# Feed-forward of an encoder block by a Strassen scheme: seven half-size products for eight, in two phases

## The reference, cut to what matters

```python
h = x + mixer(rmsnorm(x, norm1_g))              # attention and gated linear attention: not changed
n = rmsnorm(h, norm2_g)
gate = conv3(n @ w_gate) + conv_b               # depthwise over 3 neighbouring rows
h = h + (silu(gate) * (n @ w_up)) @ w_down      # w_gate, w_up 2048x5632, w_down 5632x2048
out = rmsnorm(h, final_norm_g)
```

## Time and profile before

| | |
|---|---|
| median of 3 runs | 2384.5 us (2384.22 to 2385.77) |
| span of the profiled execution | 2383.3 us (no other time of that execution is given) |
| PE busy | 98% of the span |
| DVE, ACT, POOL busy | 41%, 30%, 2% |
| DMA | 222.43 MB, mean 93 GB/s |
| last matmul of the mixer starts | 913.12 us |
| first feed-forward slab starts | 923.06 us |

### The profile page before, as it was taken

One profiled execution on the slowest core, in us unless ns is written; L12 is line 12 of the kernel. 1 busy time (PEld: TensorE's weight loads), 2 busy tenths in 40 slices (PEclk: granted clock), 3 DMA queues, 4 the chain that ended last, 5 costly groups with the idle time before them and its releaser, 6 DMA issues.

```text
span 2383.3 us, 26573 instructions
## 1 busy us (share of the span) xinstructions
PE 2340.9 (98%) x10613; PEld 1916.7 (80%) x10613; DVE 975.3 (41%) x1333; ACT 719.1 (30%) x930; POOL 39.7 (2%) x48
## 2 busy tenths in 40 slices
PE   6999999999999999999999999999999999999997
PEld 5887888887777787888888888888888888888886
DVE  4223444643564436343343434343433434343434
ACT  5224443423343233331222222221312222222214
POOL 1000000000000000000000000000000000000002
PEclk9999999999999999999999999999999999999999
DMA  5332212222242232333333232333333323223233
GB/s 174 98 96 82 62 54 71 63 79 80 80 150 67 75 97 73 114 98 97 97 97 95 94 95 96 96 97 97 97 97 97 97 97 95 94 95 95 96 97 106
DMA packets 113488, 222.43 MB, mean 93 GB/s; under 512 B 6862, under 2 KB 9140, under 8 KB 112788
## 3 DMA queue, kind: packets, MB, share of 16 engines
q1 hardware_dynamic: 111684, 215.07, 29.0%
q0 software_dynamic: 1744, 6.52, 0.8%
HBM read 217.37 MB, written 4.19 MB: 93 GB/s over the span
## 4 chain that ended last, share of the span: by engine, by line
PE 96%; ACT 1%; DVE 1%; DMA 1%; issue 0%; SPq 0%; ACTq 0%; DVEq 0%
PE dense L508 59%; PE side L508 30%; PE side L681 1%; PE side L664 1%; PE side L628 1%; PE side L624 1%; PE side L546 1%; DMA xin<-in_x 1%; PE side L671 1%; PE side L611 1%; PE side L568 0%; PE side L592 0%; PE side L640 0%; ACT L910 0%; PE side L581 0%
## 5 line engine op out<-in xcount | busy, mean ns | idle before, releaser
L1104 DVE TENSOR_TENSOR w_lo<-raw,w_hi 128x1024 fp32r<-128x1024 f32 x388 | 476.7, 1229 | 1068.1 <-ACT w_hi L843 1066.2
L843 ACT ACTIVATE w_hi<-raw 128x1024 fp32r<-128x1024 f32 x388 | 411.4, 1060 | 1241.5 <-PE dense L508 763.4
L508 PE MATMUL dense<-xT_hi,w_hi 128*128 128x512 f32 x1232 | 486.4, 395 | 0.0
L508 PE MATMUL dense<-xT_hi,w_lo 128*128 128x512 f32 x1232 | 480.2, 390 | 0.0
L508 PE MATMUL dense<-xT_lo,w_hi 128*128 128x512 f32 x1232 | 480.2, 390 | 0.0
L508 PE MATMUL side<-xT_hi,w_hi 128*128 128x512 f32 x704 | 273.9, 389 | 0.0
L508 PE MATMUL side<-xT_lo,w_hi 128*128 128x512 f32 x704 | 273.9, 389 | 0.0
L508 PE MATMUL side<-xT_hi,w_lo 128*128 128x512 f32 x704 | 273.9, 389 | 0.0
L508 PEld LDWEIGHTS dense<-xT_hi,w_hi 128*128 128x128 f32 x1232 | 231.8, 188 | 51.7 <-issue 4.8
L508 PEld LDWEIGHTS dense<-xT_hi,w_lo 128*128 128x128 f32 x1232 | 231.6, 188 | 48.8
L508 PEld LDWEIGHTS dense<-xT_lo,w_hi 128*128 128x128 f32 x1232 | 231.9, 188 | 47.6 <-issue 1.2
(11 more groups left out here) (189 smaller groups left out, 2131.4 us busy)
## 6 DMA issues: line engine op xcount, KB each, us to landing
raw<-in_w_in SPq DMA_DIRECT2D x98, 512.0 KB, 3.6
raw<-in_w_gate SPq DMA_DIRECT2D x88, 512.0 KB, 3.5
raw<-in_w_up SPq DMA_DIRECT2D x88, 512.0 KB, 3.5
raw<-in_w_down SPq DMA_DIRECT2D x88, 512.0 KB, 3.7
raw<-in_w_out SPq DMA_DIRECT2D x32, 512.0 KB, 3.7
xin<-in_x SPq DMA_DIRECT2D x4, 1024.0 KB, 9.8
hid<-in_x POOLq DMA_DIRECT2D x4, 1024.0 KB, 11.0
out<-hid SPq DMA_DIRECT2D x8, 512.0 KB, 4.4
```

The lines of the kernel that those rows point to most:

```text
L508: mm = pe.matmul(o, lhs, rhs, start=first and k == 0, stop=last and k == 2)
L843: act.activation(w_hi[slot][:, :], raw[slot][:, :], ACT.Copy).then_inc(hi_done, 1)
L1104: dve.tensor_tensor(w_lo[slot][:, :], raw[slot][:, :], w_hi[slot][:, :].bitcast(F32), ALU.subtract)\
```

## The change

**Strassen (Winograd's form).** Each slab is now a 2x2 by 2x2 block product with blocks of 256: the x side holds 2 k-tiles of 128 by 512 rows as two halves, the weight side 2 k-tiles by 512 columns as two halves. `HP` is 256, `NB` 7. Of each side four blocks and sums of blocks, seven in use, are made (`b_sums` on DVE for weights: one op of 512 elements, two of 256, each of the first two waited for by `link`), then split into hi and lo over 7 x 256 = 1792 elements (`f_split` on ACT, `f_rest` on DVE). PE does 7 products x 2 halves x 3 = 42 matmuls of 256 columns for each slab, each product into a PSUM bank of its own. At the end of a pass (8 slabs for gate or up, 5 or 6 for down) DVE forms the four result blocks by 7 operations of 512 elements that read the banks (`combine`), after ACT has saved the first bank (`save_u1`). PE's next pass waits, product by product, until its bank was read (`FREED`).

**Two phases.** Phase 1 does all gate and up passes (11 groups); the x side (8 slots of hi and lo sums) is made once, in the first pass, from turned tiles (`fill_xs`, the sums on DVE for 2 and on POOL for 6 slots, `fill_slot`, `slot_rest`). Of each group the convolution reads SBUF; POOL multiplies silu(gate) by up (4 operations of 512 elements) and forms the activations' block sums (4 operations of 512), and SP writes the 2 MB of a group to DRAM (`store_act`). Phase 2 does down in 4 chunks of the 22 hidden pairs x 4 column blocks = 16 passes; the pair's sums come back from DRAM (`load_pair`, 0.9 MB), and are split again (`refill_slot` on ACT, `refill_rest` on DVE, 1792 elements each). h itself goes to DRAM and back (`spill`, `load_res`). POOL adds `u1`, `u2`, `u3` to the result blocks (4 operations of 512 per pass).

**Also:** the feed-forward is written out in full (no hardware loop), and the final norm runs once over all rows, after the last pass. The diff, cut:

```diff
-GROUP = 2 * NSL + 2 * (D // BLK)
+HP = 256
+NB = 7
+PAIRS = KT // 2
+SLOTS = 7
+CHUNKS = [range(0, 6), range(6, 12), range(12, 17), range(17, 22)]
+PRODUCTS = ((0, 0), (2, 2), (5, 5), (4, 4), (3, 3), (6, 1), (1, 6))
+FREED = (0, 1, 2, 3, 5, 6, 7)
...
+            at.setdefault(min(freed[q] + 3, f + i - 4), []).append(q)
...
+            def load_ffn(f):
+                slot = f % RING
...
+                    sp.wait_ge(f_lo_done, f - RING + 1)
+                sp.dma_start(ksplit(stage[slot][:, 0:4 * HP], BLK), ffn_slab(f)).then_inc(stage_in[slot], 16)
...
+            for f in range(RING, NF):
+                load_ffn(f)
+                p, i = SLABS[f]
+                what, g, _, f0 = PASSES[p]
+                if what == "up" and g and i == 1:
+                    store_act(g - 1)
...
+                for q in REFILL.get(f - 2, ()):
+                    load_pair(q)
+            for h in range(2):
+                t = slice(2 * h, 2 * h + 2)
+                for done, j, last in ((fin_act, 0, 1), (fin_done, 2, 1), (fin_act, 1, 2), (fin_done, 3, 2)):
+                    sp.wait_ge(done, 4 * h + 2 * last)
+                    sp.dma_start(out_t[:, t, j * BLK:(j + 1) * BLK], res[j][:, t, :]).then_inc(stored, 16)
...
+            for g in range(NG):
+                pool.wait_ge(comb_done, NB * (2 * g + 2))
+                for m in range(G):
+                    pool.wait_ge(silu_done, G * g + m + 1)
+                    pool.tensor_tensor(cv[:, m, :], cv[:, m, :], comb[:, m, :], ALU.mult).then_inc(mul_done, 1)
+                pool.wait_ge(mul_done, G * (g + 1))
+                pool.tensor_tensor(C[:, 0, 0], A[:, 0, 0], A[:, 1, 0], ALU.add).then_inc(act_summed, 1)
...
+                for n, (a, b) in enumerate(PRODUCTS):
+                    if first and p:
+                        if n == 0:
+                            pe.wait_ge(u1_done, p)
+                        else:
+                            pe.wait_ge(comb_done, NB * (p - 1) + FREED[n])
...
+                    for m in range(2):
...
+                        for z, (lhs, rhs) in enumerate(trio):
+                            mm = pe.matmul(o, lhs, rhs, start=first and m == 0 and z == 0, stop=last and z == 2,
+                                           skip_group_check=True)
...
+            def f_split(f):
+                ring = f % RING
+                act.wait_ge(t_done, f + 1)
+                if f >= RING:
+                    act.wait_ge(f_slab, f - RING + 1)
+                act.activation(f_hi[ring][:, :], stage[ring][:, HP:], ACT.Copy).then_inc(f_hi_done, 1)
...
+            def b_sums(f):
...
+                dve.wait_ge(stage_in[ring], 16 * (f // RING + 1))
+                link(dve.tensor_tensor(half(t[:, 4 * HP:6 * HP], HP), t[:, 0:HP].unsqueeze(1).to_broadcast([P, 2, HP]),
+                                       half(t[:, HP:3 * HP], HP), ALU.subtract))
+                link(dve.tensor_tensor(t[:, 6 * HP:7 * HP], t[:, HP:2 * HP], t[:, 5 * HP:6 * HP], ALU.subtract))
+                dve.tensor_tensor(t[:, 7 * HP:8 * HP], t[:, 6 * HP:7 * HP], t[:, 3 * HP:4 * HP], ALU.subtract)\
+                    .then_inc(t_done, 1)
+            def f_rest(f):
...
+                dve.wait_ge(f_hi_done, f + 1)
+                dve.tensor_tensor(f_lo[ring][:, :], stage[ring][:, HP:], f_hi[ring][:, :].bitcast(F32), ALU.subtract)\
+                    .then_inc(f_lo_done, 1)
...
+            for f in range(NF):
+                if f + 3 < NF:
+                    b_sums(f + 3)
+                if i == len(pairs) - 1:
+                    combine(p)
+                if f + 2 < NF:
+                    f_rest(f + 2)
+                if p == 0 and 2 + i < PAIRS:
+                    slot_rest(2 + i)
+                if what == "up" and 1 <= i < 1 + G:
+                    taps(g, i - 1)
+                for q in REFILL.get(f, ()):
+                    refill_rest(q)
```

More of the change, by code:

```diff
@@ L79, with passes, refills @@
 FF0 = WA0 + HALF * (D // BLK)
-GROUP = 2 * NSL + 2 * (D // BLK)
 RING = 3
+HP = 256
[5 more added lines that the diff above has]
+FREED = (0, 1, 2, 3, 5, 6, 7)
+def passes():
+    out, f = [], 0
+    for g in range(NG):
+        for what in ("gate", "up"):
+            out.append((what, g, range(PAIRS), f))
+            f += PAIRS
+    for c in CHUNKS:
+        for j in range(D // BLK):
+            out.append(("down", j, c, f))
+            f += len(c)
+    return out
+PASSES = passes()
+SLABS = [(p, i) for p, (_, _, pairs, _) in enumerate(PASSES) for i in range(len(pairs))]
+NF = len(SLABS)
+P2 = 2 * NG
+LASTP = len(PASSES) - 1
+def refills():
+    last = {k: (P2 - 1) * PAIRS + k for k in range(SLOTS)}
+    freed, at = {}, {}
+    for p, (what, j, pairs, f) in enumerate(PASSES):
+        if what == "down" and j == 0:
+            for i, q in enumerate(pairs):
+                freed[q] = last[q % SLOTS]
+                at.setdefault(min(freed[q] + 3, f + i - 4), []).append(q)
+        if what == "down" and j == D // BLK - 1:
+            for i, q in enumerate(pairs):
+                last[q % SLOTS] = f + i
+    return freed, at
+FREE_AT, REFILL = refills()
 START = {name: IN0 + NSL * b for b, (name, _, _) in enumerate(IN_BLOCKS)}
@@ L353, in mixer_slab, with ffn_slab @@
             return w_out_t[:, t:t + KS, j * BLK:(j + 1) * BLK]
[L356 to L375, removed]
+        def ffn_slab(f):
+            p, i = SLABS[f]
+            what, g, pairs, _ = PASSES[p]
+            src = {"gate": w_gate_t, "up": w_up_t, "down": w_down_t}[what]
+            return src[:, KS * pairs[i]:KS * (pairs[i] + 1), g * BLK:(g + 1) * BLK]
@@ L377, in ksplit, with half @@
         def ksplit(t, n):
             return t.rearrange("p (k c) -> p k c", c=n)
[L380 to L398, removed]
+        def half(t, n):
+            return t.rearrange("p (m c) -> p m c", c=n)
@@ L826, in _ @@
+            for f in range(NF):
+                strassen_slab(f)
         @block.scalar
@@ new lines, in _ @@
+            for kt in range(4):
+                fill_xs(kt)
+            for kp in range(2):
+                fill_slot(kp)
+            for kt in range(4, 6):
+                fill_xs(kt)
+            for f in range(NF):
+                p, i = SLABS[f]
+                what, g, pairs, _ = PASSES[p]
+                turns = p == 0 and 3 + i < PAIRS
+                if i == len(pairs) - 1:
+                    save_u1(p)
+                if turns:
+                    fill_xs(2 * (3 + i))
+                if f + 2 < NF:
+                    f_split(f + 2)
+                if p == 0 and 2 + i < PAIRS:
+                    fill_slot(2 + i)
+                if turns:
+                    fill_xs(2 * (3 + i) + 1)
+                if what == "up" and i == 0:
+                    centre(g)
+                if what == "up" and 2 <= i < 2 + G:
+                    silu(g, i - 2)
+                for q in REFILL.get(f, ()):
+                    refill_slot(q)
+                if p > LASTP - 3 and i == 2:
+                    final_squares(g - 1)
```

679 lines of the change are left out of this document (374 added, 305 removed).

## The result

The changed kernel takes 2393.4 us (median of 6 runs, 2391.4 to 2395.5), the kernel before 2384.7 in runs beside it: ratio 1.0035, 95% interval 1.0024 to 1.0047. It is slower, by 8.7 us. The forecast was 2364, faster by 20; 2393.4 lies inside the range of 2325 to 2420, but on the side to which the prediction gave 0.32.

A forecast was written before the change was run, and what follows sets the result against it. PE, 98% busy, was taken to bound the kernel, with DVE's loaded total close to it. First slab 929.6 + pass 0 51.3 + 256 slabs 1290.2 + stalls 70 + tail 21.7 = 2362.8, forecast 2364 us, range 2325 to 2420.

The forecast's parts named there:

- The spacing: PE's Strassen matmuls of 256 columns start 120 ns apart, 42 of them making 5.04 us a slab.
- rivals of 109 and of 127 to 135 ns: PE's matmul spacing: 109 ns, faster, 2344 us, chance 0.08; or dearer than the line, 2479 at 135 ns, chance 0.15.
- Start, pass 0, tail: Outside the later slabs: first slab at 929.6 us, pass 0 takes 51.3, tail after the last matmul 21.7.
- The lock: DVE and POOL on SBUF: DVE stands still 1.2 us per POOL operation, 106 us for groups, 36 for phase 2 adds.
- Taking turns: Start of gate passes: DVE and POOL operations assumed to alternate on the lock; the forecast's own case, chance 0.42.
- The sum of the stalls: PE's stalls after pass 0, in gate and down passes and small ones elsewhere: 70 us together.
- the others 6, 6 and 2: Down chunks 1 to 3, where a combine meets refills: PE stalls of 6, 6 and 2 us.
- small stalls elsewhere 2: Remaining small PE stalls outside the gate passes and the refill zones: 2 us.
- 12 to 16, I take 12: First refills of down, coinciding with the last taps and last POOL group: PE stall of 12 to 16 us, 12 taken.
- hidden, by 2: store_act's 2 MB, issued in step 4 of the gate pass, lands near 39, before the combine needing it at 41.
- 4.2 a group: Gate passes: PE stalls of 1.0 and 3.2 us in each of ten groups, 42 us in all.
- POOL runs through: Rival, slower: POOL's operations go one after another, 6.9 us lost a gate pass, 2400 us; chance 0.18.

The follow-up runs named there:

- e9: e7 with POOL's adds of u1 to u3 in phase 2 moved to DVE, two in each of two steps: 2335.7 us, ratio 0.9796.
- e5: Changed kernel with POOL's adds of phase 2 cut to one column, so output is not the reference's: 2378.7 us, one run.
- e4: Changed kernel with the loads of res for column blocks 2 and 3 moved behind later slab loads on SP's queue: 2388.0 us, ratio 1.0012.
- e7: Changed kernel with the edits of e3 and e4 together: 2337.5 us, ratio 0.9804.
- e11: Changed kernel with 18 unused matmuls of 256 columns put into PE's longest waits in gate and down passes: 2396.0 us, ratio 1.0047.
- e12: e7 with the same 18 added matmuls at the same places as e11: 2363.9 us, ratio 0.9911.
- e1: Changed kernel with POOL's eight operations of each group cut to one column, so activations are not computed: 2339.7 us, one run.
- e3: Changed kernel with POOL's eight operations of each group moved to DVE, two behind each of four steps of the next gate pass: 2345.9 us, ratio 0.984.
- e10: e2 with store_act cut to a 32nd for every group but the first, so output is not the reference's: 2348.0 us, one run.
- e2: Changed kernel with POOL's eight operations of each group held back and spread over steps of the next pass: 2387.5 us, ratio 1.0011.
- e6: e2 with the 2 MB store of the activations issued one slab load earlier: 2390.2 us, ratio 1.0022.
- e8: e7 with POOL's third and fourth add of a down pass each held back by a slab count: 2337.9 us, ratio 0.9802.

## Why the forecast went wrong

**The spacing: right.** 42 matmuls 120 ns apart, 5.04 a slab, in all passes. The Trainium skill's "TensorE: Matmul & The Clock Gate" gives N / 2.4 + 2.5 ns in its Back-to-back issue gap, 109 at 256 columns, for a matmul by itself; this case's trace, with 120 in a stream, does not agree, as the earlier trace rows said before. The rivals of 109 and of 127 to 135 ns fall.

**Start, pass 0, tail: right in their sums.** 929.4 for 929.6; 52.0 for 51.3; 22.1 for 21.7. Inside pass 0 the waits are others than forecast: PE waits 5.2 us in four places for ACT's fills of `xs`, where the prediction had 4 for POOL's sums.

**The lock: right in kind, and in sum by luck.** DVE stood still for 140 us where the prediction had 142. The group cost 90 for 106 and the adds of phase 2 32 for 36. Some 7 in the first pass (POOL's sums for the x side) and 9 in the last passes (twelve operations in which POOL multiplies by the final norm's factors) were in no term, and they fill up the sum; e9, with neither group nor adds on POOL, still has them (the five groups sum to 998 for 982). "Taking turns" was an assumption, and the timeline shows it, one POOL operation for one DVE operation, four a step. "SBUF — State Buffer", Who interferes with whom, in the Trainium skill, has the exclusive lock; the trace agrees, at 1.02 us an operation of the group, where the rule would give the 1.3 that one lasts by itself.

**The sum of the stalls: wrong, and it decided.** The step said 70; 97.8 were lost, and break-even lay at 90. Three of its terms were too small. The first alone decides the sign: with POOL's adds left out (e5, one run) the kernel takes 2378.7, less than the one before.

1. *Down, "the others 6, 6 and 2" and "small stalls elsewhere 2"*: 27.5 for 16 (26.3 in chunks 1 to 3, 1.2 in the up passes). The prediction counted 36 us for POOL's adds in DVE's total, and put none of them into a place. e5 shows what they cost PE there: 16.1. Without them chunks 1 to 3 lose 10.2, so the terms for the refills alone were not too small.
2. *Chunk 0, "12 to 16, I take 12"*: 24.2, of which 9.3 are slabs 185 and 186. The prediction called the store "hidden, by 2", and that holds for the ten stores that stand in the gate passes. It did not follow SP's queue to the last one, with a load behind it that waits until the store has landed. e4 and e7 show what this cost in the time: 5.4 and 8.4. The other 14.9 of chunk 0 lie in the 12 to 16 of the prediction.
3. *The gate passes, "4.2 a group"*: 46.0 in ten for 42. The waits are smaller than forecast (34.2; 0.8 and 2.5 in a pass for 1.0 and 3.2), but 12.0 more go by behind them, about 11 of it at the lower clock. The prediction had a cold clock in pass 0 alone, and no term for one behind a stall. Over the whole kernel it is about 20 us. e11 and e12 forbid calling these a cost that could be had back by keeping PE busy: with the clock kept up, other waits come for it.

The rival "POOL runs through" has a time close to the measured one, 2400, and not its mechanism: it needs 6.9 a gate pass, with POOL's operations one after another, and the passes lose 4.6, with turns taken.

**What stayed open.** The stalls fall when DVE has less to stand still for (e1, e3, e5) or a queue is freed (e4, e7, e10), and hardly when work is moved in time (e2, e6, e8), when an add goes to DVE at the same price (e9), or when PE is kept busy (e11, e12). That the lateness is handed on to the next step without cover (the time by which a load or a DVE result is there before it is needed) is shown for the store (e2, e10). For the steps of chunks 1 to 3 in which refills stand, 10.2 us with the adds off, it is only read from the timeline. Why the clock stayed up behind two of ten equal waits (2.3 us, in the first and the ninth of these gate passes) stays open.

## What to carry to other kernels

When two engines share a lock, charge the one that sets the pace for the other's operations, in the steps where they fall, and ask what they would cost on that engine itself: for the group 0.64 against 1.02, and the move turned +0.35% into -1.6%; for the adds 0.64 against 0.54, and the move gave 1.8 us. A stall that was spread or filled came back here at the next place where cover was just enough, so list the covers that are short by a few us, above all the loads behind a store, before moving work. And follow each queue to its last element: one load that waits for a store to land holds up all that stand behind it.

## What the runs showed of the hardware

- With a queue on both, DVE and POOL alternated operation by operation, one POOL operation of 512 elements for one of DVE, whether that takes 0.42, 0.69 or 2.02 by itself; POOL's own took 1.29 alone, 2.94 across an `f_rest`.
- Behind the wait of 2.29 us ahead of the fourth slab of a gate pass, 12 to 15 steps between matmuls of 256 columns were 213 ns in eight of the ten passes, and 120 ns thereafter. 213.3 is 256 / 1.2, so the 13.3 ns that each costs at 2.4 GHz are not added at 1.2. Behind the waits of 0.6 the spacing was 120 but for the first step of 220.
- The load of 512 KB that follows a 2 MB store of phase 1 on SP's queue took 6.1 to 7.7 us to land in the changed kernel, 6.0 to 8.8 in e2 and 8.1 to 9.2 in e6, and 3.5 to 4.8 behind the cut stores of e10; the median of its group is 3.6 in the changed kernel.
